# First block's attention: turned probabilities in more than one buffer, and each head's output product issued one turn later

## The reference, cut to what matters

```
logits = q @ k.T * HEAD_DIM ** -0.5        # 512 x 512, causal, and only keys that an index selected
p      = softmax(logits)                   # float32
y      = p @ v                             # 512 x 128 for each head
```

## Time and profile before

| what | value |
|---|---|
| time, median of 3 runs | 1853.41 us (1851.26 to 1854.27) |
| span of the profiled execution, first to last instruction | 1844.9 us |
| the profiled execution's own time | not listed apart from its span |
| mean granted clock of TensorE over the span | 0.946 of full speed |
| TensorE busy with matmuls | 89% of the span |
| the attention stage on PE, first S to first `gb` matmul | 419.5 to 483.9 us |

### The profile page before, as it was taken

How to read it: one execution, slowest core, us unless ns; L and a number is a source line. 1 busy time by engine, 2 the same in 40 slices (tenths; PEclk the granted TensorE clock), 3 DMA queues, 4 the chain that set the end, 5 groups by cost and what they waited for, 6 DMA issues and landing times.

```text
span 1844.9 us, 19448 instructions
## 1 busy us (share of the span) xinstructions
PE 1643.1 (89%) x7716; PEld 1056.7 (57%) x7716; DVE 835.0 (45%) x1356; ACT 345.9 (19%) x574; POOL 247.1 (13%) x295
## 2 busy tenths in 40 slices
PE   5996999998899698788599997998969998999997
PEld 4685888775688533333388885776833333333333
DVE  6899745525346421111642328875442323233333
ACT  3310100115300211111210137564100000000001
POOL 0102002300000131110200004674020000000000
PEclk9999999999999799899799997888979999999998
DMA  4232132220044799999522200002789999999993
GB/s 169 79 99 84 46 106 100 92 69 23 26 156 183 283 354 419 427 427 422 202 103 69 90 25 1 1 1 92 288 295 416 430 430 428 431 429 430 432 430 165
DMA packets 51878, 403.69 MB, mean 219 GB/s; under 512 B 12608, under 2 KB 13888, under 8 KB 22608
## 3 DMA queue, kind: packets, MB, share of 16 engines
q1 hardware_dynamic: 44368, 389.86, 52.6%
q0 software_dynamic: 7424, 12.61, 1.9%
HBM read 398.21 MB, written 16.81 MB: 225 GB/s over the span
## 4 chain that ended last, share of the span: by engine, by line
PE 72%; DVE 11%; DMA 7%; ACT 4%; issue 3%; POOL 3%; SPq 0%; POOLq 0%; DVEq 0%; ACTq 0%
PE bank L1652 33%; PE bank L694 17%; PE bank L709 8%; DMA arena<-in_expert_in 3%; PE bank L673 2%; DMA ring<-in_expert_in 2%; PE bank L674 1%; DVE arena L2373 1%; PE bank L1767 1%; DMA ring<-in_stream_a 1%; DVE top L2372 1%; DVE ring_low L2268 1%; ACT misc L2024 1%; PE bank L1644 1%; PE bank L1867 1%
## 5 line engine op out<-in xcount | busy, mean ns | idle before, releaser
L694 PE MATMUL bank<-arena 128*64 128x512 f32 x960 | 278.6, 624 | 24.0 <-issue 8.0
L2267 DVE CAST ring_high<-ring 128x2048 fp32r<-128x2048 f32 x60 | 75.8, 1264 | 261.6 <-DMA ring<-in_stream_a 157.8
L694 PE MATMUL bank<-ring,arena 128*64 128x512 f32 x576 | 181.8, 610 | 9.1 <-issue 8.8
L694 PEld LDWEIGHTS bank<-arena 128*64 128x64 f32 x960 | 85.0, 143 | 171.9 <-issue 169.4
L1066 DVE TENSOR_TENSOR resid<-resid,bank 128x512 f32<-128x512 f32 x120 | 81.8, 685 | 204.7 <-PE bank L674 204.7
L2268 DVE TENSOR_TENSOR ring_low<-ring,ring_high 128x2048 fp32r<-128x2048 f32 x60 | 140.8, 2347 | 2.1
L709 PE MATMUL bank<-arena 128*64 128x512 f32 x448 | 116.0, 603 | 8.2 <-issue 5.9
L1652 PE MATMUL bank<-ring_low,xn_high 128*128 128x512 f32 x288 | 113.3, 393 | 0.0
L1652 PE MATMUL bank<-ring_high,xn_high 128*128 128x512 f32 x288 | 112.6, 391 | 0.0
L1652 PE MATMUL bank<-ring_high,xn_low 128*128 128x512 f32 x288 | 112.6, 391 | 0.0
L694 PEld LDWEIGHTS bank<-ring,arena 128*64 128x64 f32 x576 | 55.5, 140 | 68.2 <-issue 68.2
(11 more groups left out here) (387 smaller groups left out, 3084.2 us busy)
## 6 DMA issues: line engine op xcount, KB each, us to landing
ring<-in_stream_a SPq DMA_DIRECT2D x42, 1024.0 KB, 5.0
arena<-in_expert_gate SPq DMA_DIRECT2D x20, 2048.0 KB, 17.5
arena<-in_expert_in SPq DMA_DIRECT2D x18, 2048.0 KB, 24.5
arena<-in_expert_up SPq DMA_DIRECT2D x18, 2048.0 KB, 19.6
arena<-in_expert_down SPq DMA_DIRECT2D x18, 2048.0 KB, 20.5
ring<-in_expert_up SPq DMA_DIRECT2D x12, 2048.0 KB, 22.3
ring<-in_expert_down SPq DMA_DIRECT2D x12, 2048.0 KB, 19.3
ring<-in_expert_gate SPq DMA_DIRECT2D x12, 2048.0 KB, 19.9
```

What stands on the lines that cost most here:

```text
L694: last = nc.tensor.matmul(h[side * SLOTS:(side + 1) * SLOTS, :], tokens[:, k, side * SLOTS:(side + 1) * SLOTS], w[:, k * 512:(k + 1) * 512 ...
L2267: then(V.tensor_copy(hi, ring_raw[n % RING]))
```

## The change

A head's O product, and ACT's copy of it, move one turn later. PE's turn h now holds S of head h, T of head h - 2 and O of head h - 3, and there is one more turn at the end. ACT's turn h holds exp of head h, Tc of head h - 1 and Oc of head h - 2. The order of the units follows. `pT` becomes several buffers: even heads use the old place; odd heads use a place that the upper half of `yT` takes later (heads 1 and 3) and a place in `qT` whose heads are through (heads 5 and 7). Tc of a head waits for O of two heads before.

```diff
-    for h in range(HEADS + 2):
+    for h in range(HEADS + 3):
         if h < HEADS:
             for t in range(NT):
                 u.add(("S", h, t), "dve")
-        if h >= 2:
+        if 2 <= h < HEADS + 2:
             for t in range(NT):
                 u.add(("T", h - 2, t), "act")
-            u.add(("O", h - 2), "act")
+        if h >= 3:
+            u.add(("O", h - 3), "act")
...
-        pT = at(arena, 5 * TILE + 1152, [NT, SEQ])
+        pT = [at(arena, 5 * TILE + 1152, [NT, SEQ]), at(arena, 6 * TILE + HALF_TILE, [NT, SEQ]),
+              at(arena, TILE, [NT, SEQ])]
+        def pT_of(g):
+            return pT[0 if g % 2 == 0 else 1 if g < HEADS // 2 else 2]
...
-            for h in range(HEADS + 2):
+            for h in range(HEADS + 3):
...
-                if h >= 2:
+                if 2 <= h < HEADS + 2:
                     g = h - 2
                     for t in range(NT):
                         pe.wait_ge(probs_ready, g * NT + t + 1)
...
+                if h >= 3:
+                    g = h - 3
                     b = begin(("O", g))
                     wait_read(pe, ("v", 1, NT - 1))
                     wait_read(pe, ("T", g, NT - 1))
...
-            for h in range(HEADS + 1):
+            for h in range(HEADS + 2):
...
-                        if t == 0 and g >= 1:
-                            act.wait_ge(psum_filled, U.filled(("O", g - 1)))
-                        read(nc.scalar.copy(pT[:, 0:t + 1, t * P:(t + 1) * P],
+                        if t == 0 and g >= 2:
+                            act.wait_ge(psum_filled, U.filled(("O", g - 2)))
+                        read(nc.scalar.copy(pT_of(g)[:, 0:t + 1, t * P:(t + 1) * P],
                                             b[:, 0:(t + 1) * P].rearrange("p (j q) -> p j q", q=P)))
+                if h >= 2:
+                    g = h - 2
                     b = unit(("O", g))
                     read(nc.scalar.copy(yT[:, g, :], b[:, :]))
```

More of the change, by code:

```diff
@@ L1767, in _ @@
                         last = nc.tensor.matmul(b[:, s * P:SEQ], v_rows[:, s, g * HD:(g + 1) * HD],
-                                                pT[:, s, s * P:SEQ], start=(s == 0), stop=(s == NT - 1))
+                                                pT_of(g)[:, s, s * P:SEQ], start=(s == 0), stop=(s == NT - 1))
                     end(last)
@@ L2025, in _ @@
                                              accum_out=sums[:, h, t:t + 1]).then_inc(exp_ready, 1)
-                if h >= 1:
+                if 1 <= h < HEADS + 1:
                     g = h - 1
```

## The result

The changed kernel took 1835.67 us (median of 5 runs, 1830.63 to 1839.38); the kernel before, with two more runs, took 1851.26 us (median of 5, 1843.71 to 1854.27). The ratio is 0.9916, 95% interval 0.9894 to 0.9937, so 15.6 us at the medians. The forecast was 1841.0 us with a range of 1838.0 to 1845.0: right in its direction, about right in the size of the gain, and too high in the time, which lies 2.3 us under the lower end of the range.

A forecast was written before the change was run, and what follows sets the result against it. PE and ACT waiting for each other in the attention stage was taken as the bound; PE's walk brought `gb` from 483.87 to 471.43, gain 12.4 us, so 1853.4 - 12.4 = 1841.0 us, range 1838.0 to 1845.0.

The forecast's parts named there:

- The ring of exp, Tc, O and Oc: Attention stage: PE and ACT wait for each other in turn, making a turn 6.63 us where PE alone needs 5.49.
- The walk, steps 1 to 7: PE's groups followed from turn 2 to the first `gb` matmul, forecast at 471.43 against 483.87 us: gain 12.4 us.
- ACT's cover of 1.3 us, step 4: Turns 4 to 7: Tc ends at 4.26 us, next O at about 5.6, so PE sets the pace, not ACT.
- DVE (3.0): Full turns: DVE's scaling ends at 4.65 us and PE needs it only after the next S, cover 3.0 us.
- The unknown seam from T to O: PE passing from T to an O that does not wait: T taken as 1.10 us; gain 12.6 cheap, 10.1 dear.
- Pass on of the whole gain: Behind the stage: nothing later has a fixed clock time, so all 12.4 us reach the kernel's time.
- the level: Whole kernel: median of runs shown lies 8.5 us above the profiled span, kept as is, so 1853.4 - 12.4 = 1841.0 us.
- the 1.5 us of scatter: Whole kernel: runs of 1851.26 to 1854.27 us taken as scatter of about 1.5 us either way, for the range.
- Half clock in the tail: Rival: PE falls to 1.2 GHz where T7 waits for DVE, or behind turn 2; time 1842.7 to 1844.6 us, chance 0.10.
- A gain swallowed later: Rival: behind the stage, a transfer does not come earlier; 1853.4 us if all is lost, about 1847 if half; chance 0.04.
- half clock through the stage: Rival: PE's clock stays below 2.4 GHz, each full turn costs 3.57 us, 1869.6 us with all eight; chance 0.02.
- ACT as the bound: Rival: ACT's turn becomes 6.0 us, five turns lose 0.5 each, time 1843.5 us; chance 0.04.

The follow-up runs named there:

- second profile of before: The kernel before, unchanged, profiled once more: 64.52 us for the stage, then 132.6 us to the first router product, span 1845.0 us.

## Why the prediction was right or wrong

**What bounds the stage: right.** The ring of exp, Tc, O and Oc set the pace. The buffers alone left it untouched, ACT's copy alone took 0.22 of the 1.22 us out of a full turn (6.41 us), and the order alone took out all of it.

**The walk, steps 1 to 7: right, 12.4 us forecast, 13.1 measured.** S3 was forecast at 434.49 and came at 434.56, T1 436.65 and 436.73, O0 437.75 and 437.82, turn 4 439.98 and 439.98, turn 8 461.94 and 461.62, T7 465.49 and 465.18, O6 466.97 and 466.66, `gb` 471.43 and 470.89. The term that was a little large is the full turn, 5.41 and not 5.49: an O that does not wait gives way after 445.39 - 443.23 = 2.16 and not 2.23. I had read the 2.23 off O products that had waited. One statement of mine was loose: SP does issue a transfer at 419.73 us, as turn 0 begins. It is ahead of all that was moved.

**ACT's cover of 1.3 us, step 4: right.** ACT now stops 1.36 us in each full turn, and 1.28 us of idle work on it cost 0.3 in all. What would be late next in a full turn was misjudged: the bank of the O unit (cover 2.0), not DVE (3.0).

**The unknown seam from T to O: right at the cheap end.** T gives way after 443.23 - 442.14 = 1.09 us (1.10 taken). The rule of the Trainium skill that spoke against it ("TensorE: Matmul & The Clock Gate", Part 3) does not hold here for loads of whole arrays: the load it would add to each seam does not show. Part 2 of the same page of the Trainium skill, on the background buffer, fits.

**Pass on of the whole gain: right.** The way from `gb` to the router took 132.5 us as before.

**The step that failed is the level, "The median of the runs shown lies 8.5 us above the profiled span, which is what lies around it", and the 1.5 us of scatter beside it.** What lies around the span is 1.9 to 2.1 us in every run whose span was listed: the changed kernel's profiled run has 1836.01 us and a span of 1833.9. The other 6.4 us were scatter: by its span the profiled execution took about 1847, and the three runs shown (1851.26 to 1854.27) were longer than most. In later runs, before had medians of 1849.36 (23 runs, 1844.97 to 1856.39) and 1849.48 (11 runs). From 1849.4 the same gain gives 1837.0, still 1.0 under the range, but a range of the same reach around it, 1834.0 to 1841.0, would hold the measured 1835.67. With the 13.1 us of the stage it gives 1836.3, beside 1835.67 and 1835.55. Three runs within 3 us of each other did not show a scatter of some 10 us.

Of the 5.3 us between 1841.0 and 1835.67, 2.15 are the level of before as the two more runs moved it (1853.41 to 1851.26), 0.7 are the stage (13.1 for 12.4), and 2.5 are what the medians show beyond the stage (15.6 for 13.1), which no experiment explains.

Where the 6.4 us lay is not shown. The stretch of the second block is one source, of 8.4 us, but the profiled execution had its long form and still was short, with 54.3 in place of 60.8 us behind it. An estimate: an execution with the long form and 60 us behind it would take 185.9 + 59.9 - 177.6 - 60.8 = 7.4 us more than the second profile of before (1847.06), or 1854.5, which is near the three runs shown. None of those three was profiled.

**The first ratio, 15.6 us, need not hold more than the stage.** The second gave 13.3, and each interval holds the stage's 13.1 (a ratio of 0.9929).

**The rivals.** Half clock in the tail did not come: O6 and O7 together take 4.48 us. It did come in other kernels, behind stops of 1.4 us in one and of 2.0 and 2.6 us in another, so its chance was not zero. A gain swallowed later, half clock through the stage and ACT as the bound did not occur.

## What to carry to other kernels

Where two engines each wait for the other inside a turn, look at the order of the instructions on each of them before adding a buffer. Here further buffers were worth nothing until the consumer had moved behind independent work, and then, by the stage's traces, only where that work runs out, in the tail. When an engine is held up on purpose, look for idle time on that engine first: it tells whether the stops of its partners matter at all. Judge a gain of under 1% by the stretch in two traces, not by a median of three runs, and read what lies around the span from an execution whose time and span are both known.

## What the runs showed of the hardware that was not expected

- O0 behind a stop of 1.36 us ran 2.40 us in the kernel before, and 3.99 us behind 1.38 in the kernel with ACT's copy later, whose instructions on PE are the same up to there. In the kernel with the order alone, O7 kept its clock (2.39 us) behind a stop of 1.65. The lower clock level is not decided by the length of the last stop alone; what decides was not settled.
- In the second block the same 850 matmuls took 177.6 or 186 us in two executions of the kernel before. The mean granted clock was 0.86 in the long one and 0.92 in the short one.
- A group of matmuls that had not waited gave way sooner: O after 2.16 us, against 2.23 behind a wait, at the same clock.
